# Input projections of a hybrid decoder step: the order of the eight input tiles within a weight unit

## What is computed

```
def swiglu(x, wi, wo):
    gt, up = jnp.split(x @ wi, 2, axis=-1)
    return (jax.nn.silu(gt) * up) @ wo
...
x = x + 0.5 * swiglu(rmsnorm(x, w['ffn1_norm'][i]), w['ffn1_wi'][i], w['ffn1_wo'][i])
...
z, xbc, dt_raw = jnp.split(u @ w_in, [D_INNER, D_INNER + CONV_DIM], axis=-1)
...
k, v = jnp.split(rmsnorm(x, kv_norm) @ w_kv, 2, axis=-1)
...
gate = jax.nn.sigmoid(rmsnorm(x, w['ple_norm'][i]) @ w['ple_gate'][i])
```

## Time and profile before

| | before |
|---|---|
| median of three runs | 1192.98 us |
| the three runs | 1192.48, 1192.98, 1193.37 us |
| span of the profiled execution, first to last instruction | 1191.4 us |
| TensorE (PE) busy | 1182.5 us, 99% |
| VectorE (DVE) busy | 867.6 us, 73% |
| ScalarE (ACT) busy | 699.4 us, 59% |
| GpSimd (POOL) busy | 245.7 us, 21% |
| HBM traffic over the span | 202 GB/s |

### The profile page before, as it was taken

How to read it: one execution, slowest core, us unless ns; L and a number is a source line. 1 busy time by engine, 2 the same in 40 slices (tenths; PEclk the granted TensorE clock), 3 DMA queues, 4 the chain that set the end, 5 groups by cost and what they waited for, 6 DMA issues and landing times.

```text
span 1191.4 us, 26530 instructions
## 1 busy us (share of the span) xinstructions
PE 1182.5 (99%) x9785; PEld 1155.5 (97%) x9785; DVE 867.6 (73%) x1377; ACT 699.4 (59%) x1149; POOL 245.7 (21%) x352
## 2 busy tenths in 40 slices
PE   9999999999999999999999999999999999999998
PEld 8999999998989899999999999999999899999998
DVE  7766645999899868677745987788468867676447
ACT  6455435787686657555545855555368765444345
POOL 1000001422222102222344323232026310000001
PEclk9999999999999999999999999999999999999999
DMA  8765554755445365867787577656743356555552
GB/s 286 253 205 181 185 181 142 261 181 192 150 160 179 119 219 179 326 222 255 266 300 245 199 270 269 236 171 231 262 156 111 98 167 211 180 185 180 177 180 86
DMA packets 63297, 239.90 MB, mean 201 GB/s; under 512 B 7672, under 2 KB 9632, under 8 KB 58848
## 3 DMA queue, kind: packets, MB, share of 16 engines
q1 hardware_dynamic: 56880, 197.83, 49.4%
q0 software_dynamic: 6064, 40.66, 9.4%
q10 hardware_dynamic: 288, 0.54, 0.1%
HBM read 226.87 MB, written 13.39 MB: 202 GB/s over the span
## 4 chain that ended last, share of the span: by engine, by line
PE 94%; DVE 3%; ACT 1%; issue 1%; DMA 1%; SPq 0%; POOL 0%; DVEq 0%; POOLq 0%; ACTq 0%
PE bank L504 29%; PE bank L505 29%; PE bank L506 29%; PE bank L874 1%; PE bank L869 1%; DVE xl L1577 1%; DVE wlo L1558 1%; PE bank L896 1%; DMA x<-xT 1%; PE bank L926 0%; ACT under L1476 0%; ACT whi L1083 0%; PE bank L682 0%; PE bank L668 0%; PE bank L876 0%
## 5 line engine op out<-in xcount | busy, mean ns | idle before, releaser
L1558 DVE TENSOR_TENSOR wlo<-raw,whi 128x1024 fp32r<-128x1024 f32 x367 | 457.2, 1249 | 237.1 <-ACT whi L1083 235.8
L504 PE MATMUL bank<-xh,whi 128*128 128x264 f32 x2008 | 576.2, 287 | 1.8 <-DVE wlo L1767 0.9
L505 PE MATMUL bank<-xl,whi 128*128 128x264 f32 x2008 | 569.2, 283 | 0.0
L506 PE MATMUL bank<-xh,wlo 128*128 128x264 f32 x2008 | 568.8, 283 | 0.0
L1083 ACT ACTIVATE whi<-raw 128x1024 fp32r<-128x1024 f32 x367 | 385.5, 1055 | 242.4 <-PE bank L506 231.0
L504 PEld LDWEIGHTS bank<-xh,whi 128*128 128x128 f32 x2008 | 378.2, 188 | 5.6 <-issue 1.4
L505 PEld LDWEIGHTS bank<-xl,whi 128*128 128x128 f32 x2008 | 378.5, 188 | 0.9
L506 PEld LDWEIGHTS bank<-xh,wlo 128*128 128x128 f32 x2008 | 376.6, 188 | 0.0
L504 PE MATMUL bank<-hh,whi 128*128 (+1 forms) x896 | 255.5, 285 | 0.0
L506 PE MATMUL bank<-hh,wlo 128*128 (+1 forms) x896 | 255.0, 285 | 0.0
L505 PE MATMUL bank<-hl,whi 128*128 (+1 forms) x896 | 254.4, 284 | 0.0
(11 more groups left out here) (333 smaller groups left out, 1012.7 us busy)
## 6 DMA issues: line engine op xcount, KB each, us to landing
raw<-weights SPq DMA_DIRECT2D x367, 512.0 KB, 3.6
under<-ssm POOLq DMA_DIRECT2D x8, 1024.0 KB, 7.7
xact<-ssm POOLq DMA_DIRECT2D x8, 1024.0 KB, 7.3
out_ssm_s<-xact POOLq DMA_DIRECT2D x8, 1024.0 KB, 5.3
xact<-dtx_rows POOLq DMA_DIRECT2D x5, 1024.0 KB, 9.9
zs<-dtx_rows POOLq DMA_DIRECT2D x2, 1024.0 KB, 14.6
x<-xT SPq DMA_DIRECT2D x4, 264.0 KB, 6.0
xact<-stat_rows POOLq DMA_DIRECT2D x2, 528.0 KB, 6.7
```

Source lines behind the costliest of these rows:

```text
L504: pe.matmul(out, whi[:, w, c], rh, start=start, stop=False)
L505: pe.matmul(out, whi[:, w, c], rl, start=False, stop=False)
L506: return pe.matmul(out, wlo[:, w, c], rh, start=False, stop=stop)
L1558: dve.tensor_tensor(wlo[:, s, :], raw[:, s, :], whi[:, s, :].bitcast(F32), ALU.subtract).then_inc(lo_ready, 1)
```

## The change

`unit_a` and `sin_unit` walk the input tiles in the order of a tuple in place of 0 to 7. The first matmul of the new order begins the accumulation, the last ends it. The waits for single input tiles in `unit_a` become one wait for all eight ahead of the loop. `unit_pair`, `first_units`, `query_unit` and all stages of the second kind are as before.

```
+FOUR_APART = (0, 4, 1, 5, 2, 6, 3, 7)
...
-                for k in range(KT):
-                    if x_wait:
-                        pe.wait_ge(xl_ready, XREADY[stage] + k + 1)
-                    if kv_wait:
-                        pe.wait_ge(kvl_ready, k + 1)
-                    mm = split_products(out[:, 0:N], s, k, rh[:, k, :], rl[:, k, :], k == 0, k == KT - 1)
+                if x_wait:
+                    pe.wait_ge(xl_ready, XREADY[stage] + KT)
+                if kv_wait:
+                    pe.wait_ge(kvl_ready, KT)
+                for k in FOUR_APART:
+                    mm = split_products(out[:, 0:N], s, k, rh[:, k, :], rl[:, k, :], k == FOUR_APART[0], k == FOUR_APART[-1])
                 mm.then_inc(unit_used, 1)
...
-                for k in range(KT):
-                    mm = split_products(out[:, 0:N], s, k, xh[:, k, :], xl[:, k, :], k == 0, k == KT - 1)
+                for k in FOUR_APART:
+                    mm = split_products(out[:, 0:N], s, k, xh[:, k, :], xl[:, k, :], k == FOUR_APART[0], k == FOUR_APART[-1])
                 mm.then_inc(unit_used, 1)
```

## The result

The changed kernel takes 1195.85 us (median of 7 runs, 1195.37 to 1197.26), the kernel before 1193.1 us in the same runs. The ratio is 1.0024, with a 95% interval of 1.0015 to 1.0033: slower by 2.8 us, with 1.8 to 3.9 us in the interval. The profiled execution took 1196.05 us, with a span of 1194.2 us. Two executions among the later runs, of 2964.34 us (old order everywhere) and 5603.68 us (best order), are slow ones and stand in none of the ratios.

The account below looks back on a forecast made before the run. TensorE's pace from matmul to matmul was taken as the bound. 1192.98 us plus 231 units x 0.012 us (+2.8 us), with nothing for waits or unit ends, gave 1195.8 us; range 1188 to 1203 us.

Parts of the forecast that it names:

- What bounds the kernel: Whole kernel: TensorE, 99% busy, sets the end by its matmul pace; pace changes go into the time almost one to one.
- The cause is where the operand starts within 256 bytes: Input projections: small differences between tile times, 0.35 to 0.38 us, go with where the moving operand starts.
- Step 2 of the sum: New tile order in 231 units of `unit_a` and `sin_unit`: time per unit u from 2.900 to 2.912 us, +2.8 us.
- the last rival: In sin, other TensorE work keeps a pattern from settling; only 184 units count, +2.2 us, 1195.2 us; no separate chance.
- The halfway value between the present pattern and three others: Time per changed unit, 2.912 us: halfway between 2.900 and 2.924, the average of f1o0 and the sin and f2i0 pairs.
- The pace given for f1o0: In f1o0, one and the same matmul shape runs at 121.1 to 123.8 ns, by the tile it reads.
- The neutral rival: Changed units: new order settles as long as the old, within 10 ns of 2.900 us; 1193.0 us, chance 0.32.
- The faster rival: Changed units: steps of 128 and 96 bytes keep reads apart, u falls to 2.87 us, 1186.0 us or 1188.4; chance 0.24.
- The waits and the end of the unit: The single kv wait costs nothing, at most 2.5 us without cover; ring and banks come free as before, nobody newly late.

Follow-up runs that it names:

- best order: Changed kernel with order 0, 2, 3, 6, 5, 4, 1, 7 instead of four apart, shifted by four tiles in f1i1; 1191.88 us, ratio 0.9990.
- The blocks: Kernel before, with 14 blocks of 96 matmuls into an unused bank ahead of its work; 120.0 to 123.3 ns per matmul at 264 columns, whole time not given.
- rotated order: Changed kernel with f1i1 alone walking its tiles 4, 0, 5, 1, 6, 2, 7, 3; 1194.39 us, ratio 1.0012.

## Why the prediction came out right, and where it did not

The forecast was 1195.8 us, slower; 1195.85 us was measured. The direction came from the argument. That the size fits to 0.1 us is luck, since the per-unit value was guessed halfway between two others and does not hold in any stage.

- **What bounds the kernel**: right. A pace of TensorE that changes by 0.2 to 1.6% per unit went into the time almost one to one, and the idle time ahead of TensorE's first product line grew by 0.4 us only.

- **The cause is where the operand starts within 256 bytes**: right, and now shown by three runs that moved only the order or only an address. The prediction left out that the weight tile's place counts as much. It set the weights aside, since they are the same; they are the fixed end from which the place is measured. The run that moved the weights shows it.

- **Step 2 of the sum, u = 2.912 us in all units**: the total was right and the distribution wrong. The settled units are 2.907 us in most stages (+7 ns) and 2.947 in f1i1 (+47 ns). By stages, 126 units at 7 ns (f1i0, f2i0 and f2i1) are 0.9 us, and 42 at 47 ns are 2.0 us, while sin gave 0.1 us where 47 x 12 ns = 0.6 were counted. So the last rival, that a pattern hardly settles in sin, was right for that stage. The halfway value between the present pattern and three others was a guess about an average, and an average over stages is what it met. With f1i1 at the places of the other stages, or in its old order, the whole takes 1194.1 to 1194.4 us (three runs), which I had called neutral. The pace given for f1o0, 121.1 to 123.8 ns, has a slip: 2.91 us over 24 are 121.3 ns. Nothing hangs on it.

- **The neutral rival** was argued with f1i0 and f1i1 having the same pace though they lie 128 bytes apart. That is so only because walking by 32 bytes passes the same closed sequence of places from either start. Four apart, shifted by 128 bytes, is another sequence.

- **The faster rival**: its mechanism (steps of 32 bytes cost, larger ones keep the reads apart) fell with the stage at a single place, 2.96 us without any step. Its premise, that a pattern faster than 0 to 7 exists, is right: 2.893 us. But 4 of 4 orders in one run and 27 of 28 in another were not faster, so the chance I left for a faster one by an arbitrary order, 0.24, was high.

- **The waits and the end of the unit**: right. The old order with the new waits is the kernel before.

- The formula of the Trainium skill, "TensorE: Matmul & The Clock Gate", section "Back-to-back issue gap", gives the gap of a single matmul by the number of columns alone; for a stream with weight loads the same section says that both operations set the spacing. The blocks are such a stream, and their spacing does not follow from the columns alone: 120.0 to 123.3 ns at one number of columns, and 11.50 us from the first block of 256 columns to the next, against 11.52 for 264 at the same place.

What stays open: by what mechanism the relative place of the moving tile and the weight tile changes the pace, what picks one of two rhythms at the same place, and what makes the granted clock fall in some executions.

## What to carry to other kernels

Where TensorE is the bound and its matmuls stand back to back, the distance of their starts, unit by unit, is worth reading to the nanosecond: the busy share says 99% in all of these kernels. If it depends on the tile, look at the addresses of moving and stationary operand within 256 bytes; a pad of 128 bytes ahead of a tensor changed the pace of one stage by 1.4% here (2.947 to 2.907 us). And measure an order or a pad in the kernel, since times per tile don't add up, and a gain in TensorE's pace is lost where the weights come no sooner. Before a microsecond is put down to a change, compare the granted clock stretch by stretch: the page's 40 slices show nine tenths or more in every run here, also in those where it fell for a few microseconds.

## What the runs showed of the hardware that was not expected

- Most settled units repeat to a nanosecond, and their lengths come in steps of 6.67 ns, which is 16 cycles at 2.4 GHz: 2.880, 2.893, 2.900, 2.907, 2.913, 2.920, 2.927, 2.933, 2.940, 2.947 and 2.960 us are 432, 434 to 442 and 444 of them. A few alternate between two values (2.901 and 2.919 us) or have a rhythm that does not close with the unit. The same order at the same places gave the same value in f1i0, f2i0, f1i1 and f2i1 in every run with a trace.

- Two fp32r matmuls with 264 moving columns start on average at least 120.0 ns apart in any settled block with its own weight load each; by the place of one operand against the other it is up to 123.3 ns, the worst at 128 bytes. With 256 columns at place 0 it was 120.0 ns as well, at place 128 it was 118.7, and with 240 columns it was 112.0.

- Over a whole stage the spread was from 2.880 us to 2.960 us per unit, 2.8%, with the same work, by addresses and order alone.

- TensorE's granted clock fell to its lower level for a few microseconds in the midst of the kernel in two of the traces, which are longer by 1.2 us there: 0.57 on average over 4 us around 948 us with the rotated order, 1.00 in the same stretch of the run with `xh2` moved.
